# Four moves in the hand-written orders of VectorE and ScalarE in a one-layer Hymba kernel

## The chip, the cores and the metric

The kernel runs on one core of one Trainium2 chip. The metric is the device time of one execution in microseconds (us), the median of several runs. The engines are called TensorE (PE in the rows, PEld its weight loads), VectorE (DVE), ScalarE (ACT), GpSimd (POOL) and SyncE (SP, which issues DMAs).

## The reference, cut to what matters

One layer of a decoder, for 1024 rows of a new sequence and 8 rows of a cached one, in float32:

```python
h = _rmsnorm(x, g_pre_mix)
aq, ak, av, rq, rf, ri, rg = jnp.split(h @ w_in, SPLIT_POINTS, axis=-1)
...
a = _swa_prompt(q, k, v, sinks)
...
f = lb + (1.0 - lb) * jax.nn.sigmoid(rf.astype(F32))
log_f = jnp.log(f).reshape(B, T, N_REC_HEADS, REC_DK)
kr = (1.0 - f).reshape(B, T, N_REC_HEADS, REC_DK)
qr = jax.nn.silu(rq.astype(F32)).reshape(B, T, N_REC_HEADS, REC_DK)
o, S_new = _hgrn2_scan(qr, log_f, kr, ir, S0)
...
mix = jnp.concatenate([a, o], axis=-1).astype(x.dtype) @ w_out
x = x + _rmsnorm(mix, g_post_mix)
h2 = _rmsnorm(x, g_pre_ffn)
ffn = (jax.nn.silu(h2 @ w_gate) * (h2 @ w_up)) @ w_down
x = x + _rmsnorm(ffn, g_post_ffn)
```

`a` is attention over a window of 128 with a sink in the softmax (8 query heads, 2 key heads of 64). `_hgrn2_scan` is a gated linear recurrence with 4 heads of 128. `lb`, the lower bound of the forget gate, comes from a softmax over `rec_lb`. The model width is 1024, the FFN's hidden width 2816.

## The kernel before, in words

Each engine runs a program that is written out in order by hand, in loops over the same counters; semaphores connect the engines. An instruction that waits holds up everything behind it on its engine, so the order within a loop is what a change of order moves.

All large products are made of float32 numbers split in a high and a low part. ScalarE copies the high part (`copy`, L1261 in the rows), VectorE subtracts it from the number to get the low part, and TensorE multiplies high by high, high by low and low by high.

**Input projection with mixer, 132 ticks.** The projection has 22 tiles of 128 columns by 3 chunks of 344 rows, 66 units; a tick is half a unit, twelve matmuls of 128x344 (L1811). Between the ticks' matmuls TensorE takes the steps of attention and of the recurrence that the tables `attention_steps(tick)` and `recurrence_steps(tick)` name. Attention runs over 32 items; on even ticks come Q, R, E, S and M, on odd ticks PT, PV, N and D:

- S is TensorE's score product (L1886), which ScalarE copies out; D on VectorE puts in the other scores, takes the maximum and ends in `tsum` (L2448). TensorE's S of an item two later waits for that (`at_max`).
- E are ScalarE's exponentials (L1458) and `esk`; N on VectorE adds up `den` (L2452) and inverts it.
- R on ScalarE is `unit_probabilities`, the scaling of the exponentials by `rden` (L1386); PT on TensorE transposes them (L1893), PV multiplies them with the values.

The recurrence takes each of the 4 heads through a product on the diagonal ("own scores", L2486) and then seven levels, one a tick, from tick 56 + 18 h for head h. At a level VectorE runs `decay` on the queries (L2386), a masked copy of the scores out of PSUM (`copy_predicated`, L2499) and `key_step` twice (L2381); between them ScalarE moves half of the keys (`mix<-hqk` and `hqk<-hqk`, L1261). TensorE's product of the next level (L1940) waits for the decay and for the move.

Units of kind rq, rf and rg pass through gates: `unit_read` on ScalarE, at the end of odd ticks, applies the tanh (for rf with an ACT_TABLE_LOAD where the table differs, L1334) and `unit_finish` on VectorE the product (L2364, and `q_s` behind the last chunk, L2368). In a tick of VectorE come first the attention steps, then `unit_finish`, then the recurrence's steps; for heads 2 and 3 the levels come ahead of `unit_finish` (`levels_first`). The lower bound is computed in tick 27 (`lower_bound`, L2281 to L2292): three instructions on `lbt`, an Exp on ScalarE, five more instructions, and the negation of one row of `gain` (L2418), all ahead of the attention steps of that tick.

**Output projection**, then the FFN's gate and up products in a scheme of seven products per block: the list `PRODS` has 154 products of 24 matmuls of 128x258 (L2069). The first 16 are P1 and P2 of columns 0 to 7; from number 16 on they come as P6, P5, P7, P3, P4 of column 0, then of column 1 and so on. VectorE reads each product out of PSUM (`ffn_read`, L2744), which frees the pair of banks for a product three numbers later, and multiplies gate and up (`hidden`, L2751).

P6, P5, P7 and P3 work on sums of blocks of rows, split once: `sum_high` on ScalarE and `sum_low` (L2678) on VectorE, two halves each, for the four sums 2, 1, 3 and 4. TensorE waits for them at column 0 only (`s_low` 2, 4, 6 and 8). The weights are brought in as jobs X, Y, Z and W: T, T3 and T4 are sums of weights on VectorE (`weight_sums`, L2603 to L2609), `job_high` on ScalarE copies the high part, `job_low` (L2594) subtracts on VectorE. Two tables say behind which product each step comes, for both engines: `early_steps(n)` for n under 16, and `weight_steps(n)` for all others, whose entry for 16 is T4 and W of column 0.

Of the kernel before, what the change touches and what calls it, by code (L numbers as in the profile page):

```python
# [11 lines left out]
ALU = mybir.AluOpType  # L12
# [152 lines left out]
def early_steps(n):  # L165

    return {0: [("X", 2)],
# [3 lines left out]
            12: [("Y", 0), ("L", 1)], 13: [("L", 3)], 14: [("T3", 0)], 15: [("Z", 0), ("L", 4)]}.get(n, [])  # L171
# [42 lines left out]
def build(nc, t_in, t_out):  # L214
# [468 lines left out]
    def query_early(tick, i):  # L683

        return ROPE_UNITS[query_unit(i)] < tick // 2 - 2

# [572 lines left out]
    def _(act):  # L1259
# [137 lines left out]
        for tick in range(TICKS):  # L1397
# [10 lines left out]
            if tick == LB0:  # L1408
                act.wait_ge(sem("lb_step"), 1)
                act.activation(lbt[:, 2:4, :], lbt[:, 0:2, :], ACT.Exp).then_inc(sem("lb_step"), 1)  # L1410
# [26 lines left out]
            for step, i in attention_steps(tick):  # L1437
# [7 lines left out]
                elif step == "R":  # L1445
# [7 lines left out]
                elif step == "E":  # L1453
                    act.wait_ge(sem("at_max"), i + 1)
                    if i >= 2:
                        act.wait_ge(sem("at_pt"), i - 1)
                    for g in range(NKV):
                        act.activation(prob[:, e, g, :], sm[:, e, g, :], ACT.Exp, bias=negm[:, e, g:g + 1], scale=SCALE,  # L1458
                                       accum_out=den[:, e, g:g + 1])
                    act.activation(esk[:, e, :], tsum[:, e, :], ACT.Exp).then_inc(sem("at_prob"), 1)  # L1460
                elif step == "PT":
                    act.wait_ge(sem("at_pt"), i + 1)
                    if i:
                        act.wait_ge(sem("at_pv"), i)
                    copy(pt_all[:], both_groups(BP[:, 0:NKV * P])).then_inc(sem("at_ptc"), 1)
                elif step == "PV":
                    act.wait_ge(sem("at_pv"), i + 1)
                    for g in range(NKV):
                        h = slice(HD * g, HD * g + HD)
                        ins = copy(mix[h, t, P * j:P * j + P], BO[h, P * g:P * g + P])  # L1470
                    ins.then_inc(sem("at_out"), 1)
            if tick == AT0:
# [77 lines left out]
            if tick % 2:  # L1550
                for step, i in attention_steps(tick + 1):
                    if step == "Q" and query_early(tick + 1, i):
                        query_rows(i)
                unit_read(tick // 2)
# [198 lines left out]
        for n in range(2 * EARLY, NPROD):  # L1753
            ffn_reads(n)
            for name, q in weight_steps(n):
                if name in "XYZW":
                    job_high((name, q))
            if n == PIX["P7", FT - 1]:
# [462 lines left out]
    def _(dve):  # L2221
# [59 lines left out]
        def lower_bound():  # L2281
# [4 lines left out]
            dve.tensor_tensor(lbt[:, 1, :], lbl[:, 1, :], lbt[:, 4, :], ALU.subtract).then_inc(sem("lb_step"), 1)  # L2286
            dve.wait_ge(sem("lb_step"), 2)
# [119 lines left out]
        for tick in range(TICKS):  # L2407
# [7 lines left out]
            if tick == LB0:  # L2415
                lower_bound()
                dve.wait_ge(sem("g_in"), 16)
                then(dve.tensor_scalar(gain[:, PRE_FFN, :], gain[:, PRE_FFN, :], -1.0, None, ALU.mult))  # L2418
# [8 lines left out]
            for step, i in attention_steps(tick):  # L2427
# [26 lines left out]
                elif step == "M" and j:  # L2454
# [4 lines left out]
                        .then_inc(sem("at_ptp"), 1)  # L2459
            if tick == 17:  # L2460
# [5 lines left out]
            levels_first = any(step[0] == "level" and step[1] >= NREC - 2 for step in recurrence_steps(tick))  # L2466
# [424 lines left out]
        for n in range(2 * EARLY, NPROD + 1):  # L2891
            ffn_reads(n)
            for name, q in weight_steps(n):
                if name in "XYZW":
                    job_low((name, q))
                else:
                    weight_sums(name, q)
            down_steps(n)
# [86 lines left out]
```

## Time and profile before

| | |
|---|---|
| median of 3 runs | 1178.89 us (1178.26 to 1178.94) |
| the profiled execution, its own time | 1179.54 us |
| its span in the trace | 1177.8 us |
| TensorE busy | 1165.0 us, 99% of the span |
| VectorE busy | 874.2 us, 74% |
| ScalarE busy | 533.7 us, 45% |
| mean granted TensorE clock | 0.998 |

Times in the rows count from the span's start. In a timeline each row is an instruction, or several equal ones in a row (x2): its start, its length, engine, line, operation, the tiles it writes and reads with their shapes, and in brackets how long its engine had been idle before it and whose work ended that idle time. An instruction may start shortly before the one ahead of it ends. A row without brackets follows its predecessor without a wait; where the engine is TensorE, the pitch from start to start then tells more than the length, since matmuls overlap.

### The profile page before, as it was taken

To read this page: it belongs to the slowest core of one execution; us is meant where nothing else is said; L and a number is where in the kernel's file an instruction comes from. 1 tells how busy PE (TensorE), PEld (TensorE's weight loads), DVE (VectorE), ACT (ScalarE), POOL (GpSimd) and SP (SyncE) were. 2 spreads that over 40 slices of the span, in tenths; PEclk is the share of its full clock that TensorE was granted. 3 is DMA by queue.
4 is the path that set the end of the run, shared out by engine and by line. 5 is a ranking of instruction groups with operands and counts; after the bars stand their busy time and mean duration, and the time that the engine had idled before them with its cause. 6 is when DMAs were issued, how large, how long until landed. Compare 5 with 4: busy or idle time off the path is not lost.

```text
span 1177.8 us, 22993 instructions
## 1 busy us (share of the span) xinstructions
PE 1165.0 (99%) x8962; PEld 1147.4 (97%) x8962; DVE 874.2 (74%) x1493; ACT 533.7 (45%) x1192; POOL 242.2 (21%) x190
## 2 busy tenths in 40 slices
PE   9999999999999999999999999999999999999998
PEld 9999999999999999999999999999999999999997
DVE  4988587776677747799777888888887565567676
ACT  6766656745253744564222322322322235455533
POOL 1000010201120000000232365765674020000011
PEclk9999999999999999999999999999999999999999
DMA  9521101006562243253454648766864286678446
GB/s 298 144 84 34 37 19 39 19 3 125 53 157 81 84 152 94 73 158 93 138 157 153 193 162 251 234 225 224 251 233 162 101 271 189 211 255 272 147 103 118
DMA packets 173548, 170.65 MB, mean 145 GB/s; under 512 B 23064, under 2 KB 125224, under 8 KB 172912
## 3 DMA queue, kind: packets, MB, share of 16 engines
q1 hardware_dynamic: 171264, 166.00, 46.8%
q0 software_dynamic: 2176, 3.18, 1.8%
q8 instruction: 72, 1.18, 0.4%
q14 instruction: 36, 0.29, 0.1%
HBM read 117.59 MB, written 52.58 MB: 144 GB/s over the span
## 4 chain that ended last, share of the span: by engine, by line
PE 86%; DVE 7%; ACT 3%; issue 2%; DMA 1%; SPq 0%; DVEq 0%; ACTq 0%
PE pair L2069 33%; PE pair L2109 17%; PE pair L1811 16%; PE pair L2028 7%; PE pair L1940 2%; PE pair L1886 1%; PE pair L2171 1%; PE pair L1901 1%; PE pair L1905 1%; DMA mix<-x_cols_dram 1%; DVE w_lo L2594 1%; PE pair L1925 1%; DVE mix L2666 1%; DMA raw<-w_in_dram 1%; PE pair L1957 1%
## 5 line engine op out<-in xcount | busy, mean ns | idle before, releaser
L2069 PE MATMUL pair<-act_hi,w_hi 128*128 128x258 f32 x704 | 199.1, 283 | 1.1 <-DVE u_tmp L2744 1.1
L2069 PE MATMUL pair<-act_lo,w_hi 128*128 128x258 f32 x704 | 198.6, 282 | 0.0
L2069 PE MATMUL pair<-act_hi,w_lo 128*128 128x258 f32 x704 | 198.6, 282 | 0.0
L2109 PE MATMUL pair<-a_ring,w_hi 128*128 128x258 f32 x1056 | 191.6, 284 | 0.5 <-DVE mix L2804 0.4
L1811 PE MATMUL pair<-act_hi,w_hi 128*128 128x344 f32 x528 | 177.0, 335 | 0.6 <-DVE act_lo L2242 0.5
L1811 PE MATMUL pair<-act_hi,w_lo 128*128 128x344 f32 x528 | 169.2, 320 | 0.0
L1811 PE MATMUL pair<-act_lo,w_hi 128*128 128x344 f32 x528 | 168.9, 320 | 0.0
L2109 PEld LDWEIGHTS pair<-a_ring,w_hi 128*128 128x128 f32 x1056 | 163.1, 189 | 1.5 <-DVE mix L2804 0.8
L1261 ACT ACTIVATE w_hi<-rawx 128x512 fp32r<-128x512 f32 (+2 forms) x97 | 68.7, 709 | 195.9 <-PE pair L2069 84.6
L2069 PE MATMUL pair<-s_hi,w_hi 128*128 128x258 f32 x528 | 149.2, 283 | 0.5 <-DVE w_lo L2594 0.5
L2069 PE MATMUL pair<-mix_r,w_hi 128*128 128x258 f32 x528 | 149.3, 283 | 0.0
L2109 PE MATMUL pair<-a_ring,w_lo 128*128 128x258 f32 x528 | 148.9, 282 | 0.0
L2069 PE MATMUL pair<-s_hi,w_lo 128*128 128x258 f32 x528 | 148.8, 282 | 0.0
L2069 PEld LDWEIGHTS pair<-act_hi,w_hi 128*128 128x128 f32 x704 | 133.0, 189 | 1.5 <-issue 1.3
L2069 PEld LDWEIGHTS pair<-act_hi,w_lo 128*128 128x128 f32 x704 | 132.8, 189 | 0.0
L2069 PEld LDWEIGHTS pair<-act_lo,w_hi 128*128 128x128 f32 x704 | 132.7, 188 | 0.1
L1811 PEld LDWEIGHTS pair<-act_hi,w_hi 128*128 128x128 f32 x528 | 99.7, 189 | 2.1 <-DVE act_lo L2242 0.8
L1811 PEld LDWEIGHTS pair<-act_lo,w_hi 128*128 128x128 f32 x528 | 99.8, 189 | 0.8
L2069 PEld LDWEIGHTS pair<-s_hi,w_hi 128*128 128x128 f32 x528 | 99.6, 189 | 0.7 <-DVE w_lo L2594 0.7
L2109 PEld LDWEIGHTS pair<-a_ring,w_lo 128*128 128x128 f32 x528 | 100.1, 190 | 0.0
L2069 PEld LDWEIGHTS pair<-mix_r,w_hi 128*128 128x128 f32 x528 | 99.7, 189 | 0.0
L1811 PEld LDWEIGHTS pair<-act_hi,w_lo 128*128 128x128 f32 x528 | 99.6, 189 | 0.0
(382 smaller groups left out, 2629.1 us busy)
## 6 DMA issues: line engine op xcount, KB each, us to landing
raw<-w_up_dram SPq DMA_DIRECT2D x26, 512.0 KB, 5.2
a_in<-h_sums SPq DMA_DIRECT2D x44, 258.0 KB, 3.3
rawx<-w_gate_dram SPq DMA_DIRECT2D x22, 512.0 KB, 5.1
w_quarter<-w_down_dram SPq DMA_DIRECT2D x44, 256.0 KB, 3.7
w_sums<-w_quarter SPq DMA_DIRECT2D x44, 256.0 KB, 4.7
rawx<-w_sums SPq DMA_DIRECT2D x44, 256.0 KB, 4.0
raw<-w_in_dram SPq DMA_DIRECT2D x18, 512.0 KB, 4.1
h_scratch<-mix SPq DMA_DIRECT2D x23, 258.0 KB, 2.1
```

Of the source, the lines that this page charges most:

```text
L1261: return act.activation(out, in_, ACT.Copy)
L1811: mm = pe.matmul(out, a[:, k, :], b[:, k, cols(c)], start=(k == 0 and s == 0), stop=(k == KT - 1 and s == 2))
L1886: mm = pe.matmul(out[:, :, k0:], a[:, e, :], b[:, :, P * (j - 1) + k0:P * (j + 1)], start=(n == 0), stop=(n == 2))
L1901: mm = pe.matmul(out, vrow[:, j, :], pt_all[:], start=True, stop=(j == 0))
L1905: mm = pe.matmul(out, v_diff[:, e, :], pt_prev[:], start=False, stop=True)
L1925: mm = pe.matmul(pair_columns(BL[a])[:, :, c], kept[:, P * c:P * c + P], own_queries(a, c), start=True, stop=True)
L1940: mm = pe.matmul(pair_columns(BL[n % 2])[:, :, c], early_keys(h, n)[:, P * c:P * c + P], late_queries(n, c), start=True, stop=True)
L1957: mm = pe.matmul(BL[c // 4][:, P * (c % 4):P * (c % 4) + P], krow[:, c, :], irow[:, c, :], start=True, stop=True)
L2028: mm = pe.matmul(bank[(slot + 2) % 4][:, 0:QW], a[:, k, :], b[:, k, quad(slot // NOUT)], start=(k == 0 and s == 0), stop=(k == KT - 1 and ...
L2069: mm = pe.matmul(pair[psum_pair(n)][:, s, 0:QW], a[:, r, half + k, :], b, start=(k == 0 and i == 0), stop=(k == 3 and i == 2))
L2109: mm = pe.matmul(dpair(mt)[:, s, 0:a.shape[1]], b[:, cut], a, start=(m == 0 and n == 0), stop=(m == HALVES - 1 and n == 2))
L2171: mm = pe.matmul(row_bank(n), a, b[:, out], start=False, stop=(m == HALVES - 1 and i == 2))
```

## The change

Four moves on VectorE and ScalarE. The orders of TensorE, GpSimd and SyncE stay as they are, and no instruction is added or removed.

A. *Bounds in parts.* Of the lower bound the three first instructions go behind the attention steps of tick 27, ScalarE's Exp behind those of tick 28, the five others behind those of tick 29, and the row of `gain` behind those of tick 31.

B. *One level ahead of a gate's product.* `levels_first` holds for level 4 of every head, which adds heads 0 and 1, ticks 60 and 78.

C. *Probabilities' scaling ahead of the forget gate.* `scaled_early(tick)` is true two ticks behind a head's step "o". Where it is, R of the tick is run at the end of the tick before, ahead of `unit_read`.

D. *Low halves of row sums later.* In `early_steps` L2, L1 and L3 move from behind product steps 11, 12 and 13 to 12, 13 and 15, and L4 from 15 to 16, where it stands behind T4 and W. Both engines follow the table (for 16 by a line of their own).

```diff
-            8: [("S", 1, 1), ("S", 3, 1)], 9: [("X", 6), ("S", 2, 1), ("S", 4, 1)], 10: [("X", 7)], 11: [("T", 0), ("L", 2)],
-            12: [("Y", 0), ("L", 1)], 13: [("L", 3)], 14: [("T3", 0)], 15: [("Z", 0), ("L", 4)]}.get(n, [])
+            8: [("S", 1, 1), ("S", 3, 1)], 9: [("X", 6), ("S", 2, 1), ("S", 4, 1)], 10: [("X", 7)], 11: [("T", 0)],
+            12: [("Y", 0), ("L", 2)], 13: [("L", 1)], 14: [("T3", 0)], 15: [("Z", 0), ("L", 3)]}.get(n, [])
...
+    def scaled_early(tick):
+        return any(("o", h) in recurrence_steps(tick - 2) for h in range(NREC))
...
-            if tick == LB0:
-                act.wait_ge(sem("lb_step"), 1)
-                act.activation(lbt[:, 2:4, :], lbt[:, 0:2, :], ACT.Exp).then_inc(sem("lb_step"), 1)
...
-                elif step == "R":
+                elif step == "R" and not scaled_early(tick):
                     unit_probabilities(i)
...
+            if tick == LB0 + 1:
+                act.wait_ge(sem("lb_step"), 1)
+                act.activation(lbt[:, 2:4, :], lbt[:, 0:2, :], ACT.Exp).then_inc(sem("lb_step"), 1)
...
+                    if step == "R" and scaled_early(tick + 1):
+                        unit_probabilities(i)
                 unit_read(tick // 2)
...
             for name, q in weight_steps(n):
                 if name in "XYZW":
                     job_high((name, q))
+            if n == 2 * EARLY:
+                sum_high(4)
...
-            if tick == LB0:
-                lower_bound()
-                dve.wait_ge(sem("g_in"), 16)
-                then(dve.tensor_scalar(gain[:, PRE_FFN, :], gain[:, PRE_FFN, :], -1.0, None, ALU.mult))
...
+            if tick == LB0:
+                bound_exponents()
+            if tick == LB0 + 2:
+                lower_bound()
+            if tick == LB0 + 4:
+                dve.wait_ge(sem("g_in"), 16)
+                then(dve.tensor_scalar(gain[:, PRE_FFN, :], gain[:, PRE_FFN, :], -1.0, None, ALU.mult))
...
-            levels_first = any(step[0] == "level" and step[1] >= NREC - 2 for step in recurrence_steps(tick))
+            levels_first = any(step[0] == "level" and (step[1] >= NREC - 2 or step[2] == 4) for step in recurrence_steps(tick))
...
+            if n == 2 * EARLY:
+                sum_low(4)
             down_steps(n)
```

`bound_exponents` holds the first three instructions of the old `lower_bound`, which keeps the five others. Line numbers in the rows of the changed order are those of the changed kernel, some 3 to 13 higher.

VectorE in tick 60, before (the last row here begins the attention steps of the next tick):

```order
L2432 TENSOR_TENSOR q_lo<-mix,q_hi 128x128
L2364 SCALAR_TENSOR_TENSOR r_q<-th,r_q 128x344
L2368 COPY q_s<-r_q 128x8
L2386 TENSOR_TENSOR hqk<-hqk,hg 128x2x16x16
L2499 COPY_PREDICATED ast<-lmask,pair 128x2x16x16
L2381 TENSOR_TENSOR hqk<-hqk,hg 128x8x32
L2381 TENSOR_TENSOR hqk<-mix,hg 128x4x2x32
L2452 TENSOR_TENSOR den<-den,esk 128x2
```

and after:

```order
L2438 TENSOR_TENSOR q_lo<-mix,q_hi 128x128
L2396 TENSOR_TENSOR hqk<-hqk,hg 128x2x16x16
L2512 COPY_PREDICATED ast<-lmask,pair 128x2x16x16
L2391 TENSOR_TENSOR hqk<-hqk,hg 128x8x32
L2391 TENSOR_TENSOR hqk<-mix,hg 128x4x2x32
L2374 SCALAR_TENSOR_TENSOR r_q<-th,r_q 128x344
L2378 COPY q_s<-r_q 128x8
L2458 TENSOR_TENSOR den<-den,esk 128x2
```

The gate's product and `q_s` moved from ahead of the level's decay, masked copy and two key steps to behind them.

VectorE at products 11 to 16, before, from the sum L2 (into `mix_r` by `s2_hi`; L1 is `act_lo`, L3 and L4 `mix_r` by `s3_hi` and `s4_hi`; L2594 are the low parts of Y, Z and W):

```order
L2678 TENSOR_TENSOR mix_r_129<-mix_51,s2_hi_126 128x4x258 x2
L2744 TENSOR_TENSOR u_tmp_156<-v1_5_149,pair0 128x516
L2594 TENSOR_TENSOR w_lo_53<-t12_153,w_hi_52 128x1024
L2678 TENSOR_TENSOR act_lo_50<-mix_51,act_hi_49 128x4x258 x2
L2751 TENSOR_TENSOR p_small_157<-u_tmp_156,p_small_157 128x516
L2678 TENSOR_TENSOR mix_r_129<-mix_51,s3_hi_127 128x4x258 x2
L2606 TENSOR_TENSOR rawx_152<-rawx_152 128x512
L2744 TENSOR_TENSOR p_pq_159<-v1_6_150,pair0 128x516
L2594 TENSOR_TENSOR w_lo_53<-rawx_152,w_hi_52 128x1024
L2678 TENSOR_TENSOR mix_r_129<-mix_51,s4_hi_128 128x4x258 x2
L2744 TENSOR_TENSOR u_tmp_156<-v1_7_151,pair2 128x516
L2609 TENSOR_TENSOR rawx_152<-rawx_152,t12_153 128x512
```

(T4, in the last row, is followed by W's low part, L2594.) After:

```order
L2757 TENSOR_TENSOR u_tmp_156<-v1_5_149,pair0 128x516
L2607 TENSOR_TENSOR w_lo_53<-t12_153,w_hi_52 128x1024
L2691 TENSOR_TENSOR mix_r_129<-mix_51,s2_hi_126 128x4x258 x2
L2764 TENSOR_TENSOR p_small_157<-u_tmp_156,p_small_157 128x516
L2691 TENSOR_TENSOR act_lo_50<-mix_51,act_hi_49 128x4x258 x2
L2619 TENSOR_TENSOR rawx_152<-rawx_152 128x512
L2757 TENSOR_TENSOR p_pq_159<-v1_6_150,pair0 128x516
L2607 TENSOR_TENSOR w_lo_53<-rawx_152,w_hi_52 128x1024
L2691 TENSOR_TENSOR mix_r_129<-mix_51,s3_hi_127 128x4x258 x2
L2757 TENSOR_TENSOR u_tmp_156<-v1_7_151,pair2 128x516
...
L2607 TENSOR_TENSOR w_lo_53<-rawx_152,w_hi_52 128x512
L2691 TENSOR_TENSOR mix_r_129<-mix_51,s4_hi_128 128x4x258 x2
```

The read `u_tmp` is now ahead of L2, and L4 went from behind Z's low part to behind T4 and W's low part.

ScalarE at the end of tick 69, before:

```order
L1261 ACTIVATE q_hi<-mix 128x128
L1334 ACT_TABLE_LOAD
L1334 ACTIVATE r_f<-r_f 128x168
L1334 ACTIVATE r_f<-r_f 128x176
L1338 ACTIVATE r_f<-r_f,lbt 128x168
L1338 ACTIVATE r_f<-r_f,lbt 128x176
L1386 ACTIVATE prob<-prob,rden 128x128 x2
L1458 ACTIVATE prob,den<-sm,negm 128x128 x2
```

and after:

```order
L1264 ACTIVATE q_hi<-mix 128x128
L1389 ACTIVATE prob<-prob,rden 128x128 x2
L1337 ACT_TABLE_LOAD
L1337 ACTIVATE r_f<-r_f 128x168
L1337 ACTIVATE r_f<-r_f 128x176
L1341 ACTIVATE r_f<-r_f,lbt 128x168
L1341 ACTIVATE r_f<-r_f,lbt 128x176
L1458 ACTIVATE prob,den<-sm,negm 128x128 x2
```

The scaling moved ahead of the forget gate's table load and its four instructions; this is the one tick where ScalarE's order differs by C.

## Rows read from the trace of the kernel before

**Rows 1.** The page's busy times of the whole span, share of it and instruction counts.

```profile
PE 1165.0 (99%) x8962; PEld 1147.4 (97%) x8962; DVE 874.2 (74%) x1493; ACT 533.7 (45%) x1192; POOL 242.2 (21%) x190
```

**Rows 2.** Timeline of VectorE, tick 27.

```profile
start us, us, engine line op out<-in xcount [idle before <-releaser]
73.54 0.15 DVE L2284 TENSOR_TENSOR lbt<-lbl 128x4 f32<-128x4 f32 x1
...
75.60 0.16 DVE L2452 TENSOR_TENSOR den<-den,esk 128x2 f32<-128x2 f32 x1
...
76.99 0.16 DVE L2448 TENSOR_TENSOR tsum<-sink,negm 128x2 f32<-128x2 f32 x1
```

**Rows 3.** Timeline of TensorE, end of tick 27 and start of 28.

```profile
76.53 0.32 PE L1811 MATMUL pair<-act_lo,w_hi 128*128 128x344 f32 x1
76.69 0.32 PE L1811 MATMUL pair<-act_hi,w_lo 128*128 128x344 f32 x1
77.30 0.47 PE L1886 MATMUL pair<-k_hi,q_hi 128*128 128x512 f32 x1 [0.30 <-DVE tsum L2448]
```

**Rows 4.** Timeline of VectorE, tick 60 and the chain of 61.

```profile
174.65 0.52 DVE L2364 SCALAR_TENSOR_TENSOR r_q<-th,r_q 128x344 f32<-128x344 f32 x1
...
175.41 0.69 DVE L2386 TENSOR_TENSOR hqk<-hqk,hg 128x512 f32<-128x512 f32 x1
...
176.67 0.42 DVE L2381 TENSOR_TENSOR hqk<-hqk,hg 128x256 f32<-128x256 f32 x1
...
179.00 0.16 DVE L2448 TENSOR_TENSOR tsum<-sink,negm 128x2 f32<-128x2 f32 x1
```

**Rows 5.** Timeline of ScalarE, tick 60, the move of the keys.

```profile
176.24 0.40 ACT L1261 ACTIVATE mix<-hqk 128x256 f32<-128x256 f32 x1
```

**Rows 6.** Timeline of TensorE, score product of tick 62.

```profile
179.60 0.39 PE L1886 MATMUL pair<-k_hi,q_hi 128*128 128x512 f32 x1
```

**Rows 7.** Timeline of VectorE, the next level's decay behind tick 78.

```profile
246.15 0.68 DVE L2386 TENSOR_TENSOR hqk<-hqk,hg 128x512 f32<-128x512 f32 x1
```

**Rows 8.** Timeline of TensorE, the level product that reads it.

```profile
246.89 1.16 PE L1940 MATMUL pair<-hqk 128*128 128x128 f32 x8
```

**Rows 9.** Timeline of ScalarE, forget gate of tick 69 and scaling of 70.

```profile
209.17 1.28 ACT L1334 ACT_TABLE_LOAD   x1
...
211.94 0.68 ACT L1386 ACTIVATE prob<-prob,rden 128x128 f32<-128x128 f32 x2
```

**Rows 10.** Timeline of TensorE, the transposes of the probabilities.

```profile
212.68 0.44 PE L1893 MATMUL pair<-ident,prob 128*128 128x128 f32 x2 [0.56 <-ACT prob L1386]
```

**Rows 11.** Timeline of VectorE, own scores of the next head.

```profile
221.82 1.29 DVE L2486 TENSOR_TENSOR ast<-pair,ident 128x512 f32<-128x512 f32 x2 [0.26 <-PE pair L1925]
```

**Rows 12.** Timeline of VectorE, products 11 to 18: L2, u_tmp, L4, W.

```profile
535.25 2.37 DVE L2678 TENSOR_TENSOR mix_r<-mix,s_hi 128x1032 fp32r<-128x1032 f32 x2
537.54 0.69 DVE L2744 TENSOR_TENSOR u_tmp<-v,pair 128x516 f32<-128x516 f32 x1
...
547.47 2.37 DVE L2678 TENSOR_TENSOR mix_r<-mix,s_hi 128x1032 fp32r<-128x1032 f32 x2
...
551.80 0.69 DVE L2594 TENSOR_TENSOR w_lo<-rawx,w_hi 128x512 fp32r<-128x512 f32 x1 [0.76 <-ACT w_hi L1261]
```

**Rows 13.** Timeline of ScalarE, the high copies of L4.

```profile
546.20 2.01 ACT L1261 ACTIVATE s_hi<-mix 128x1032 fp32r<-128x1032 f32 x2
```

**Rows 14.** Timeline of TensorE, end of product 13, product 14, P3 of column 0.

```profile
536.96 0.28 PE L2069 MATMUL pair<-act_hi,w_lo 128*128 128x258 f32 x1
538.37 0.36 PE L2069 MATMUL pair<-act_hi,w_hi 128*128 128x258 f32 x1 [1.13 <-DVE u_tmp L2744]
...
552.87 0.28 PE L2069 MATMUL pair<-s_hi,w_hi 128*128 128x258 f32 x1
```

**Rows 15.** Timeline of TensorE, the sampled rows' products in the mixer.

```profile
318.05 1.93 PE L2000 MATMUL pair<-q_s,st 128*128 128x1 f32 x16
```

**Rows 16.** Windows: us, engines' busy time, granted TensorE clock, DMA share, GB/s.

```profile
core 0: us, PE busy (x) PEld busy (x) DVE busy (x) ACT busy (x) POOL busy (x), PEclk, DMA share, GB/s
320.40:323.00 2.60, 2.60 (x12) 2.60 (x11) 1.34 (x2) 1.16 (x2) 0.00 (x0) 0.50 1.15 38
...
536.00:539.00 3.00, 1.87 (x16) 1.70 (x15) 3.00 (x4) 3.00 (x5) 0.00 (x0) 1.00 0.92 245
```

More of the change, by code:

```diff
@@ L2279, in _, with bound_exponents @@
         row_angles(0)
-        def lower_bound():
+        def bound_exponents():
             dve.wait_ge(sem("const_in"), NCONST)
@@ L2286, in lower_bound @@
             dve.tensor_tensor(lbt[:, 1, :], lbl[:, 1, :], lbt[:, 4, :], ALU.subtract).then_inc(sem("lb_step"), 1)
+        def lower_bound():
             dve.wait_ge(sem("lb_step"), 2)
```

## The prediction

> **What bounds the kernel now.** I read the page's busy times first. TensorE is busy for 1165.0 us of a span of 1177.8, VectorE for 874.2, ScalarE for 533.7 [rows 1]. All that better order can give back is therefore TensorE's idle time, 12.8 us in several pieces, and each part of this change must be judged at one place: which wait ends last there, and what is late behind it. So I read the timelines of the engines around each place that the diff names, and look in each for two things: a bracket, which says that an engine stood still and for whom, and the slack between an instruction's end and the start of the one that needs it.
>
> The profiled execution took 1179.54 us, 0.65 above the median of the runs, 1178.89. I make the sum against 1179.54 and carry the difference over to the median. A measurement of this kernel can tell about 0.2% (2.36 us) from no change; "same" below means within that.
>
> **Part A, bounds in parts (ticks 27 to 31).** In tick 27 VectorE's nine small instructions, eight on lbt and one on gain, stand from 73.54 to 75.60 ahead of den and of the softmax chain that ends in tsum at 76.99 + 0.16 = 77.15 [rows 2]. TensorE's score product waits for that chain: it starts at 77.30 with 0.30 idle, though the matmul ahead of it started at 76.69 and the pitch there is 0.16 [rows 3]. With eight of the nine behind the chain, and the three of tick 27 behind it too, the chain ends up to 75.60 - 73.54 = 2.06 earlier, and the score product starts at 76.69 + 0.16 = 76.85. That is **-0.45**. The bracket alone gives -0.30 for the other end. The exponential on ScalarE moves behind a score copy and the five remaining VectorE instructions go into tick 29, behind the chain of that tick. By the share of five in nine of those 2.06 they take about 1.1 us, and VectorE enters tick 28 about 2 us ahead, which covers them. If that cover were gone they would give back those 0.45 at the next score product, no more.
>
> **Part B, one level ahead of a gate's product (ticks 60 and 78).** Here VectorE runs r_q's gate product and q_s (174.65 to 175.41, 0.76 us) ahead of the level's decay, masked copy and two key steps [rows 4]. The change puts the 0.76 us behind the key steps, as the order shows. What does the level win? Its first key step starts at 176.67, right when ScalarE's move of the keys (176.24 + 0.40 = 176.64) is done [rows 4, 5]. ScalarE does not wait for VectorE's decay there, so the key step stays at 176.67: the decay and the copy end 0.76 earlier, and VectorE then stands idle for that time. The 0.76 us come after the key steps instead, ahead of den and the chain to tsum. Tsum ended at 179.00 + 0.16 = 179.16 [rows 4], and now ends at 179.93. The score product of tick 62 starts at 179.60 without a bracket [rows 6]; with the 0.15 from tsum's end to the product that rows 2 and 3 show (77.15 to 77.30) it can start at 180.08. That is **+0.48** for head 0; without any slack it would be +0.77.
>
> In tick 78 the pattern repeats for head 1, and the work that ends last is the next level's decay: it starts at 246.15, and with its 0.68 us ends at 246.83 [rows 7]; TensorE's level product starts at 246.89 [rows 8], so nothing lies between. The 0.77 goes through whole: **+0.77**, or +0.5 if TensorE finds the slack that it had for head 0. A gain would need the decay or the copy to be what somebody waits for in these two ticks, and no row here shows that.
>
> **Part C, probabilities' scaling ahead of a forget gate.** The order of ScalarE differs in one place only, tick 70: the title's second tick has no scaling step. There the scaling (0.68) starts at 211.94, behind a table load of 1.28 us and the gate's four instructions that began at 209.17 [rows 9]. TensorE's transposes wait for it, 0.56 us [rows 10]. Moved ahead of the table load, it is done 2.8 us sooner and the wait is gone. But ScalarE's exponentials stay where they are: the gate, put 0.68 later, ends when the scaling ended before. So all that hangs on the exponentials, the next score product's chain among it, comes no sooner, and TensorE runs into it. Later VectorE's own scores, at 221.82, waited for TensorE for 0.26 [rows 11]; what TensorE gains beyond that VectorE no longer follows. I take that row, **-0.26**, between 0 (VectorE and ScalarE decide everything behind) and -0.56 (the whole bracket).
>
> **Part D, low halves of the row sums later (products 11 to 20).** L2, L1, L3 and L4 are pairs of VectorE subtractions, 2.37 us a pair (pitch 2.29); each needs a pair of copies on ScalarE of 2.01 us [rows 12, 13]. Before, L2 began at 535.25, and the read u_tmp that frees a PSUM pair stood behind it at 537.54 [rows 12]. Product 14 waited for that read: it starts at 538.37, where its predecessor's last matmul started at 536.96 and the pitch is 0.12 [rows 14]. So 1.41 - 0.12 = 1.29 is lost, and the change removes it: u_tmp starts at 535.25, TensorE does not wait, and every later product is due 1.29 earlier. P3 of column 0, which needs L4, was at 552.87 [rows 14] and is due at 551.58.
>
> What is late next is L4. Before, it started at 547.47 and was over at 549.84, 3.0 us ahead of P3 [rows 12, 14]. Now it stands behind T4 and the weights' low part W, whose w_lo started at 551.80 [rows 12]. Taking L4's pitch of 2.29 out ahead of it, w_lo starts at 549.51 at the earliest, and L4, 0.61 later (w_lo takes 0.69 and the next instruction starts 0.08 before its end), ends at 550.12 + 2.37 = 552.49: already 0.9 behind P3's new due time. It will be later than that, because L2 also filled VectorE's wait for ScalarE's high copy of Y, which now shows: w_lo of W, with nothing to fill its wait, stood 0.76 idle [rows 12], and I take 0.67 for Y: that 0.76 less the 0.09 by which an instruction starts before its predecessor's end. So w_lo of W starts at 549.51 + 0.67 = 550.18, and ScalarE, whose copy of W's high part has to be over before that, can begin L4's two high copies at about 550.05 and ends them 2.01 later, at 552.06 [rows 13]. The second subtraction, half of 2.37, then runs from about 552.3 to 553.5, and with the 0.15 to TensorE P3 starts at 553.65 instead of 552.87. Behind a wait TensorE's first matmul takes 0.08 longer (0.36 against 0.28 [rows 14]). So the wait of 1.29 at product 14 goes and one of about 2.1 at P3 takes its place: **+0.85**. The bounds are -0.24 (L4 ends at 552.49, P3 at 552.63) and +1.2 (L3, for which I find 0.36 us of slack, is late too). Queued behind L4 on VectorE are the reads of the main loop; they start about when they did before relative to TensorE, so I charge nothing for them.
>
> **The sum.** -0.45 + 0.48 + 0.77 - 0.26 + 0.85 = **+1.4 us**: the profiled 1179.54 becomes 1180.93, the median 1178.89 becomes **1180.3**. TensorE's own queue, POOL's and SP's are in the same order before and after, and no DMA is moved, so nothing else is charged. With each bound at its low end the sum is -0.30 + 0.48 + 0.5 - 0.56 - 0.24, about -0.1; at its high end -0.30 + 0.77 + 0.77 + 0 + 1.2 = 2.4. Against the median that is 1178.8 to 1181.3, the forecast's own range.
>
> **The rivals.**
> 1. **L4 is in time and D pays whole.** If ScalarE runs ahead more than I replay, P3 is not held and D is -1.29. Sum -0.75: **1178.1**. For it speaks that L4 had 3.0 us to spare; against it, that the earliest end by rows is already behind the due time.
> 2. **B costs nothing.** If the keys are moved earlier than at 176.24, the key steps come sooner and the 0.76 fits in. The sum without B's 1.25 is +0.14: **1179.0**. Against it: ScalarE's queue ahead of that move is not touched.
> 3. **All four do what they say.** -0.45 - 0.26 - 1.29 and B nothing is -2.0, with C whole -2.3: **1176.6 to 1176.9**, the edge of what counts as faster. It needs rivals 1 and 2 at once.
> 4. **Slower: TensorE's clock falls at P3.** In the stretch from 320.40 to 323.00, soon after sixteen matmuls of one column that took 1.93 us [rows 15], the granted clock is 0.50 (1.2 GHz); from 536 to 539, around the wait of 1.13 at product 14, it is 1.00 (2.4 GHz) [rows 16]. The new wait at P3 is about 2.1, longer than the one at product 14. If the clock falls for as long as it did there, 2.60 us at half speed lose 1.30, and the time is **1181.6**, slower by over 0.2%. It decides if the chip answers the wait at P3 as it answered the stretch of small matmuls and not as it answered product 14. The Trainium skill says on "TensorE: Matmul & The Clock Gate", in "A second HAM failure mode: psum-queue depth-cycling", that small idles between groups of matmuls can be enough to bring the lower level back again and again. By that rule the time would be this rival's; the trace does not bear it out at product 14.
>
> **Chances.** Forecast 0.43; rival 1 0.17; rival 2 0.16; rival 3 0.11; rival 4 0.13. Rival 3 is left out of the range, and so is what lies above rival 4's time: 1177.6 to 1181.7. Faster by over 0.2% (below 1176.53) is about two thirds of rival 3, 0.07. Slower (above 1181.25) is most of rival 4, 0.11, and the upper tail of the forecast, 0.03: 0.14. The rest, 0.79, is within 0.2%.
>
> **What would show it.** A is right if the score product near 77 us has no bracket. B is wrong if the key step of tick 60 starts before 176.6, right if VectorE idles some 0.8 us ahead of it and the score product and the level product come later by 0.5 and 0.8. C is right if the transposes near 212 us have no wait. D is right if product 14 starts without a wait and P3 of column 0 shows about 2 us of waiting for mix_r; it is wrong if P3 has none, and rival 4 holds if the granted clock behind P3 is 0.50.

## The result, and the profile after

The changed kernel takes 1181.27 us (median of 18 runs, 1179.06 to 1182.76), the kernel before on the same chips 1179.13 (18 runs, 1177.86 to 1181.57): the medians lie 2.1 us apart. The ratio on record is **1.0015, 95% interval 1.0009 to 1.0021**, 1.8 us (1.1 to 2.5) slower. The forecast was 1.4 us slower and within 0.2%. The profiled execution took 1181.22, its span 1179.4 against 1177.8.

Busy times of the changed kernel, and what TensorE waited for (engine, line and work waited for: us in all, times, longest):

```profile
PE 1165.5 (99%) x8962; PEld 1147.9 (97%) x8962; DVE 871.1 (74%) x1493; ACT 533.9 (45%) x1192; POOL 243.1 (21%) x190
```

```profile
PE pair L2076 <- DVE mix_r L2691: 2.0, 1, 2.0
PE pair L1947 <- issue: 2.0, 3, 0.8
PE pair L1824 <- DVE neg L2276: 1.1, 1, 1.1
PE pair L1947 <- DVE hqk L2396: 0.8, 1, 0.8
```

TensorE's busy time is within 0.5 us of what it was [rows 1]; what differs is its waits. Before, it had 1.13 for u_tmp and 0.56 for the probabilities [rows 14, 10]. Both are gone, and two others stand there: 2.0 for mix_r, which is L4, and 0.8 for the decay of a level, which is B.

To see where each part paid or cost, I took the start of every TensorE matmul in a profiled execution and subtracted the start of the same matmul in that of before. This difference runs level over long stretches and steps at a few places. The table gives the steps in us (negative is gained): the level behind a place less the level ahead of it, each the median over the matmuls of the stretch. It has the changed kernel and most of the experiments below ("first keys" and "next keys" are TensorE's two waits of 0.8 at the levels near 169 and 236). Steps under 0.1 us, a step of 0.2 near 534 in B alone, those of the first 45 us, where every execution differs, and what a lower clock near 320 to 350 cost or spared some executions are left out.

| place (us in the trace of before) | changed | B alone | D alone | L4 back | read alone, A, C | + keys, B | + keys, T | + keys, T, B |
|---|---|---|---|---|---|---|---|---|
| 77, A | -0.53 | 0 | 0 | -0.53 | -0.53 | -0.53 | -0.53 | -0.53 |
| 168, first keys | 0 | 0 | 0 | 0 | 0 | -0.81 | -0.81 | -0.82 |
| 172, behind them | 0 | 0 | 0 | 0 | 0 | +0.13 | +0.14 | +0.13 |
| 179, B of head 0 | +0.54 | +0.55 | 0 | +0.56 | 0 | 0 | +0.19 | 0 |
| 186, in every kernel | +0.32 | +0.30 | +0.29 | +0.31 | +0.28 | +0.28 | +0.31 | +0.27 |
| 212, C | -0.78 | 0 | 0 | -0.78 | -0.78 | -0.78 | -0.78 | -0.78 |
| 215 and 231, given back | +0.52 | 0 | 0 | +0.53 | +0.57 | +0.52 | +0.54 | +0.55 |
| 235, next keys | 0 | 0 | 0 | 0 | 0 | -0.82 | -0.82 | -0.82 |
| 239 and 247, B of head 1 | +0.78 | +0.78 | 0 | +0.78 | 0 | +0.15 | +0.55 | +0.13 |
| 340, a load | 0 | +1.12 | 0 | +0.84 | +2.77 | +3.01 | +1.66 | 0 |
| 537 and 541, product 14 | -1.39 | 0 | -1.39 | -1.36 | -1.16 | -1.20 | -1.21 | -1.23 |
| 553, P3 (product 19) | +2.28 | 0 | +2.26 | 0 | 0 | 0 | 0 | 0 |
| 558, product 21 | 0 | 0 | 0 | +1.62 | +0.76 | +0.80 | +0.19 | +0.19 |
| 594 and 616 | 0 | 0 | 0 | +0.82 | 0 | 0 | 0 | 0 |
| 645 to 651 | -0.56 | -0.60 | -0.52 | -0.52 | -0.60 | -0.52 | -0.73 | -0.73 |

The steps of the changed kernel that belong to its four parts add up to -0.53 + 0.54 - 0.78 + 0.52 + 0.78 - 1.39 + 2.28 = +1.4. The rows at 186 and 645 stand in every kernel, also in D alone, whose order is that of before up to product 11, near 530: they belong to the one profiled execution of before and not to the change. They and the row at 340 are taken up in the last section.

The lines that answer to [rows 2, 3], VectorE and TensorE at A's place: the chain to tsum runs first, lbt behind it, and the score product follows the pitch without a bracket.

```profile
74.98 0.45 DVE L2454 TENSOR_TENSOR tsum<-sink,negm 128x2 f32<-128x2 f32 x1
75.35 0.15 DVE L2291 TENSOR_TENSOR lbt<-lbl 128x4 f32<-128x4 f32 x1
...
76.59 0.32 PE L1818 MATMUL pair<-act_hi,w_lo 128*128 128x344 f32 x1
76.75 0.39 PE L1893 MATMUL pair<-k_hi,q_hi 128*128 128x512 f32 x1
```

Those that answer to [rows 4 to 8], VectorE, ScalarE and TensorE at B's places:

```profile
174.52 0.72 DVE L2512 COPY_PREDICATED ast<-lmask,pair 128x512 f32<-128x512 uint8 x1
176.05 0.42 DVE L2391 TENSOR_TENSOR hqk<-hqk,hg 128x256 f32<-128x256 f32 x1 [0.81 <-ACT mix L1264]
...
177.00 0.50 DVE L2374 SCALAR_TENSOR_TENSOR r_q<-th,r_q 128x344 f32<-128x344 f32 x1
...
175.61 0.40 ACT L1264 ACTIVATE mix<-hqk 128x256 f32<-128x256 f32 x1
...
179.44 0.47 PE L1893 MATMUL pair<-k_hi,q_hi 128*128 128x512 f32 x1 [0.30 <-DVE tsum L2454]
...
247.68 0.49 PE L1947 MATMUL pair<-hqk 128*128 128x128 f32 x2 [0.81 <-DVE hqk L2396]
```

VectorE idles 0.81 ahead of the key step of tick 60, until ScalarE's move (175.61 + 0.40) is done; the gate's product follows the key steps, and the score product and the level product both have a wait that they did not have.

Those that answer to [rows 9 to 11], ScalarE, VectorE and TensorE from C's place to the score product near 231:

```profile
209.32 0.69 ACT L1389 ACTIVATE prob<-prob,rden 128x128 f32<-128x128 f32 x2
...
213.67 0.36 ACT L1264 ACTIVATE sm<-pair 128x256 f32<-128x256 f32 x1
...
213.79 0.16 DVE L2458 TENSOR_TENSOR den<-den,esk 128x2 f32<-128x2 f32 x1 [3.93 <-ACT esk L1460]
...
214.07 0.44 DVE L2449 COPY_PREDICATED sm<-tri,pair 128x256 f32<-128x256 int32 x1
...
221.86 1.28 DVE L2499 TENSOR_TENSOR ast<-pair,ident 128x512 f32<-128x512 f32 x2
...
230.58 0.16 DVE L2454 TENSOR_TENSOR tsum<-sink,negm 128x2 f32<-128x2 f32 x1
...
212.23 0.38 PE L1900 MATMUL pair<-ident,prob 128*128 128x128 f32 x2
...
215.50 0.47 PE L1893 MATMUL pair<-k_hi,q_hi 128*128 128x512 f32 x1
...
230.89 0.47 PE L1893 MATMUL pair<-k_hi,q_hi 128*128 128x512 f32 x1
```

The transposes have no wait. The softmax chain behind them starts with den, which waits 3.93 for the exponentials' last step as it did before, and its copy of the scores (sm, done at 213.67 + 0.36 = 214.03) is ready only 0.04 before the chain takes it up.

Those that answer to [rows 12 to 14], VectorE, ScalarE and TensorE from W to P3:

```profile
550.99 0.69 DVE L2607 TENSOR_TENSOR w_lo<-rawx,w_hi 128x512 fp32r<-128x512 f32 x1 [0.76 <-ACT w_hi L1264]
551.95 2.38 DVE L2691 TENSOR_TENSOR mix_r<-mix,s_hi 128x1032 fp32r<-128x1032 f32 x2 [0.26 <-ACT s_hi L1264]
...
550.86 2.01 ACT L1264 ACTIVATE s_hi<-mix 128x1032 fp32r<-128x1032 f32 x2
...
537.87 0.28 PE L2076 MATMUL pair<-act_hi,w_hi 128*128 128x258 f32 x1
...
554.47 0.36 PE L2076 MATMUL pair<-s_hi,w_hi 128*128 128x258 f32 x1 [2.03 <-DVE mix_r L2691]
```

Product 14 starts at 537.87 without a wait. L4 ends at 551.95 + 2.38 = 554.33, and P3 starts 0.14 later.

### The profile page after: what moved, and what is told of

It reads as the page before. It is cut to its first block, busy times and chain, and to the rows that moved or that the text cites. A ratio compares the mean times of both kernels' runs of the same rounds, so it can differ in the third digit from the quotient of the medians.

```text
span 1179.4 us, 22993 instructions
## 1 busy us (share of the span) xinstructions
PE 1165.5 (99%) x8962; PEld 1147.9 (97%) x8962; DVE 871.1 (74%) x1493; ACT 533.9 (45%) x1192; POOL 243.1 (21%) x190
## 4 chain that ended last, share of the span: by engine, by line
PE 82%; DVE 9%; ACT 4%; issue 2%; DMA 1%; SPq 0%; DVEq 0%; ACTq 0%
PE pair L2076 33%; PE pair L2116 17%; PE pair L1818 14%; PE pair L2035 7%; PE pair L2178 1%; PE pair L1947 1%; PE pair L1893 1%; DVE w_lo L2607 1%; DMA mix<-x_cols_dram 1%; PE pair L1908 1%; PE pair L1912 1%; DVE mix L2679 1%; DVE hqk L2391 1%; DMA raw<-w_in_dram 1%; PE pair L1964 1%
```

## The experiments

Each kernel is the one named with the edit shown. Times are medians beside runs of the kernel before on the same chip; the steps by place are in the table.

**D alone.** The kernel before with the change's lines of `early_steps`, `sum_high(4)` and `sum_low(4)` only.

> Kernel before with part D alone. Theory (the read moved ahead removes one wait, L4 behind W makes another): the wait of 1.13 at product 14 is gone, and P3 of column 0 waits about 2.0 us for mix_r, as in the changed kernel; TensorE is 1.3 ahead between the two and about 0.8 behind after P3; the time is 0.5 to 0.9 us over that of before. Rival (B's and C's delays upstream are what makes L4 late): without them P3 waits under 1 us and the time is at least 0.5 us under before.

Measured: ratio 1.0005 (0.9994 to 1.0016). By place it is what the theory says: -1.39 at product 14, then 2.02 of waiting for mix_r, +2.26. That is +0.87, with nothing upstream changed, so the rival falls. The runs alone do not decide it: their interval, 0.7 us under to 1.9 over, holds the theory's 0.5 to 0.9 over and the rival's 0.5 under.

**B alone.** The kernel before with one line:

```diff
-step[1] >= NREC - 2 for step
+(step[1] >= NREC - 2 or step[2] == 4) for step
```

> Kernel before with part B alone. Theory (the gate's product now stands between the key steps and the softmax chain, and nothing waited for the level): the key step of tick 60 starts no sooner than 0.03 after ScalarE's move of the keys, with some 0.8 us of VectorE idle ahead of it, TensorE loses 0.4 to 0.5 at the score product near 179.6, some 0.2 to 0.3 at the next near 186 and 0.8 at the level product near 246.9; the time is about 1.4 us over before. Rival (B is covered, and the loss of the changed kernel is all D's): the time is within 0.4 us of before.

Measured: ratio 1.0010 (1.0000 to 1.0021). By place +0.55 at the score product near 179 and +0.78 at the level product, 1.33 in all, so the rival falls. The +0.30 at the next score product, near 186, is not B's: D alone has +0.29 there.

**L4 back ahead of W.** The changed kernel with

```diff
-15: [("Z", 0), ("L", 3)]}
+15: [("Z", 0), ("L", 3), ("L", 4)]}
```

and without its two lines for 16.

> The changed kernel with only L4 put back behind L3, ahead of T4 and W, on both engines. Theory (the place of L4 in the two queues makes the wait at P3): product 14 has no wait, P3's wait shrinks from 2.0 to under 0.3, and the time is 1.3 to 2.0 us under that of the changed kernel. Rival (VectorE has too much to do between products 11 and 19, whatever its order): P3, P7 or P4 waits 1 us or more instead, and the time is within 0.7 us of the changed kernel.

Measured: ratio 1.0009 (0.9999 to 1.0019), so no gain on the changed kernel's 1.0015 that the intervals show. P3 has no wait, as the theory says, but product 21 does, for the low part of Y of column 1:

```profile
560.19 0.39 PE L2074 MATMUL pair<-s_hi,w_hi 128*128 128x258 f32 x1 [1.33 <-DVE w_lo L2605]
```

Another 0.8 is lost near 594 and 616. L4's place makes the wait at P3, and yet the rival had the time right: in this order too VectorE has more to do from product 14 to 21 than there is time for, and the wait is handed on.

**Less work for VectorE.** The kernel just shown, with L1's low halves taken for the first of four blocks of rows; the other three quarters are left out.

```diff
-1: (mix[:, 4:8, rows], act_hi[:, 0:4, rows], act_lo[:, 0:4, rows]),
+1: (mix[:, 4:5, rows], act_hi[:, 0:1, rows], act_lo[:, 0:1, rows]),
```

> The kernel with L4 put back ahead of T4 and W (the run before of that kind waited 1.3 us for Y's low part at product 21), and with L1's two subtractions on a quarter of their rows' blocks, so that VectorE has about 1.6 us less to do between products 12 and 21; three quarters of L1's low halves are left out. Theory (from product 14 on VectorE's queue is full to product 21, so a wait only moves along it): the wait at product 21 is under 0.2 us and no other appears between products 14 and 21. Rival (Y of column 1 is late for ScalarE or a load, not for VectorE's work): the wait at product 21 stays above 1 us.

Measured in one execution: no wait of TensorE is left between product 14 and product 21; the step at product 14 stays whole, -1.36. So it was the amount of work in VectorE's queue that made product 21 wait, and the theory stands. (The time of this one execution, 1186.8, is that of the wait near 340 and a fall of the clock behind it.)

**Only the read ahead of L2, with A and C, without B.** The kernel before with A, C and

```diff
-11: [("T", 0), ("L", 2)], 12: [("Y", 0), ("L", 1)],
+11: [("T", 0)], 12: [("L", 2), ("Y", 0), ("L", 1)],
```

> Kernel before with A, C and another form of D: only the read of product 11 goes ahead of L2, all four sums otherwise in the places of before; B left out. Theory: A gives 0.45, C 0.2 to 0.3, the read 1.3 and P3 has no wait, 2.0 us in all at that point; further on, the wait of 0.6 at the product near 645 may grow, since VectorE does not come sooner there. The time is 1.0 to 2.2 us under before. Rival (a wait further on takes all of it back): within 0.6 us of before.

Measured: ratio 0.9995 (0.9981 to 1.0009), undecided. By place A (-0.53), C (-0.21) and the read (-1.16) give about what was expected and P3 has no wait, but product 21 gives back 0.76 (L4 back had a wait there too), and in the profiled execution a wait of 2.6 near 340, which stands in other kernels too, took more than all of it.

**Exponentials ahead of the gate as well.** The changed kernel, with E of tick 70 run behind R at the end of tick 69.

> The changed kernel, with ScalarE's exponentials of tick 70 moved ahead of the forget gate too, behind the scaling. Theory (C's gain is cut at the next score product because the exponentials stay behind the gate): the score product near 215.5 has no wait any more, where the changed kernel gave back 0.23; the gain of 0.6 at the transposes stays. Rival (the copy of the scores or VectorE's chain behind cuts it): the score product near 215.5 gives back 0.2 as in the changed kernel.

Measured in one execution: the theory falls. TensorE gives back 0.40 at the score product near 215, as the changed kernel does (0.38), and VectorE shows for whom it waits now:

```profile
212.40 0.17 DVE L2469 RECIPROCAL rden<-den 128x2 f32<-128x2 f32 x1
213.93 0.45 DVE L2459 COPY_PREDICATED sm<-tri,pair 128x256 f32<-128x256 int32 x1 [1.36 <-ACT sm L1264]
```

The reciprocal behind den comes 1.6 us sooner than in the changed kernel, and then the chain waits for ScalarE's copy of the scores, the third step that stands behind the gate. In the changed kernel the exponentials and this copy are ready almost together, so moving the exponentials alone gains nothing; the copy alone was not tried.

**All three ahead of the gate.** The same with S of tick 70 ahead too.

> The changed kernel with all of ScalarE's attention steps of tick 70 ahead of the forget gate: scaling, exponentials and score copy. In the run with only the exponentials ahead VectorE waited 1.36 us for the score copy. Theory (the score copy behind the gate is what cuts C's gain): the score product near 215.5 gives back under 0.1; the chain on VectorE of the head behind decides again near 230.7, where 0.2 to 0.5 is given back. Rival (the gate, now 1 us later, holds its own readers): TensorE shows a new wait between 212 and 225.

Measured in one execution: the score product near 215 gives back nothing (+0.02), and C's -0.78 is held to 220, but then +0.15 before 225, +0.38 at the transposes near 228 and +0.32 at the score product near 231 take all of it back. The theory on the copy stands. By place C's net gain is -0.26 in the change and -0.25 with the exponentials ahead, and there is none with all three ahead (+0.09). This execution also shows rival 4 of the prediction (below).

**Keys moved early, with B.** The kernel with A, C and the read alone; ScalarE runs its move of the keys of levels 2 and 4 just ahead of E instead of behind the attention steps; and B.

```diff
 elif step == "E":
+    for other in recurrence_steps(tick):
+        if other[0] == "level" and moved_early(tick, other[2]):
+            key_move(other[1], other[2])
```

> Kernel before with A, C, the read alone ahead of L2, and B, and with ScalarE's move of the keys ahead of the exponentials at the levels 2 and 4. Theory (B lost because the key step waits for that move in ScalarE's queue; and the two waits of 0.8 at the levels near 169 and 236 are that move as well): with B the key step of tick 60 starts 0.6 to 0.8 sooner than in the changed kernel, B's losses at the score products near 179 and 186 and at the level product near 247 shrink to under 0.3 in all, and the two waits near 169 and 236 lose 0.6 or more each. Rival (VectorE's gate product ahead of the softmax chain is what costs, whenever the keys come): B's losses stay at 1.2 or more.

Measured in one execution (its time of 1183.17 holds the wait near 340 and a fall of the clock behind it): the two waits near 169 and 236 are gone (-0.81, -0.82), and the +0.54 at 179 and the +0.78 at 247 that B cost are gone as well. VectorE's key step follows the copy without a wait:

```profile
174.03 0.72 DVE L2521 COPY_PREDICATED ast<-lmask,pair 128x512 f32<-128x512 uint8 x1
174.64 0.40 DVE L2400 TENSOR_TENSOR hqk<-hqk,hg 128x256 f32<-128x256 f32 x1
```

What is left, 0.13 near 172, 0.28 at 186 and 0.15 near 239, is over the 0.3 that was expected, but it stands in the next kernel too, which has no B. The rival falls: the move of the keys was what the levels waited for.

**Keys early and T a product earlier, without B.** The kernel with A, C, the read alone and the keys early, and in `weight_steps`

```diff
-plan = {-3: ("T", "Y"), -1: ("T3", "Z"), 0: ("T4", "W")} if q else
+plan = {-4: ("T",), -3: ("Y",), -1: ("T3", "Z"), 0: ("T4", "W")} if q else
```

> Kernel before with A, C, the read alone ahead of L2, ScalarE's move of the keys ahead of the exponentials at the levels 2 and 4, without B, and with the weights' sum T of columns 1 to 7 one product earlier than Y, so that VectorE has a read to do while ScalarE copies Y's high part. Theory: A 0.45, C 0.2, the keys 1.2 to 1.6, the read 1.2, and the wait at product 21 that the read alone brought (0.5 to 0.7) is gone; 2.5 to 3.5 us under before, less up to 0.7 further on. Rival (VectorE's full queue gives back the read's 1.2 further on, and the keys' gain is cut by the chains behind): less than 1.2 us under before.

Measured: ratio **0.9980 (0.9971 to 0.9989)**, 2.4 us (1.3 to 3.4) under before. That is just under the 2.5 that the theory had at the least, and the rival, less than 1.2, falls. Product 21 gives back 0.19 instead of 0.76: with a read between T and Y VectorE stands still for 0.59 instead of 1.19 while ScalarE copies Y's high part.

**The same with B.**

> The kernel that was 0.2% faster (A, C, the read alone ahead of L2, keys moved early on ScalarE at the levels 2 and 4, T a product earlier) with B added. Theory (once the keys come early B no longer waits, and spares TensorE the 0.5 at the level product near 247): by place the losses at 172, 180, 186 and 247 fall from 1.1 to about 0.5; 0.4 to 0.7 us under that kernel apart from the wait near 340, that is 2.5 to 3.5 us under before. Rival (B costs 1.2 wherever it stands): about 1.2 us over that kernel.

Measured: ratio **0.9974 (0.9963 to 0.9985)**, 3.1 us (1.8 to 4.4) under before, the fastest kernel here. From 172 to 247 TensorE loses 0.54, where the kernel without B loses 1.19: with the keys early B gains 0.6, where in the change it costs 1.3. The interval overlaps that of the kernel without B, so between these two the places decide, not the runs.

**The same with tick 70's steps ahead of the gate.**

> The same kernel with ScalarE's attention steps of tick 70 all ahead of the forget gate. Theory: like it, and 0.2 us less at the score product near 215; 2.5 to 3.7 us under before. Rival (given back near 230.7): equal to it within 0.2 us by place.

Measured: ratio 0.9984 (0.9975 to 0.9993). By place -0.78 at 212, nothing at 215, and +0.36 and +0.33 at 228 and 231: the rival is right, the gain is given back there.

## Why the forecast held, point by point

*Part A* was forecast at -0.45, and the score product's first matmul comes 0.45 sooner. The step is -0.53, since the first matmul behind a wait takes 0.08 longer; the prediction counted that 0.08 in D, and not in A and B. A's remainder, moved to ticks 29 and 31, shows up nowhere.

*Part B*: the mechanism is right in each step: the key step waits for ScalarE's move, VectorE idles 0.81 (0.76 forecast), the gate's product falls into the softmax chain. Head 0 was forecast at +0.48 and is +0.54, the same 0.08 included; head 1 was forecast at +0.77 and is +0.78. *Rival 2*, that B costs nothing, was bound to a key move earlier than 176.24; in the changed kernel it is not, and with the move made earlier B did pay.

*Part C* was forecast at -0.26 and is -0.78 + 0.52 = -0.26. The mechanism is the one forecast: den still waits for the exponentials, so 0.38 is given back at the score product near 215. The rest follows VectorE, whose queue shows no wait from 221.86 to tsum at 230.58. Before, VectorE had idled 0.26 for TensorE at 221.82 [rows 11]; that idle stretch is gone, it was all that VectorE could win, and at 231 TensorE gives back what it had beyond that. Two things were missed without harm. The gain at the transposes is more than the bracket of 0.56, which the prediction took for the most that there was. And the copy of the scores holds the chain as long as the exponentials do, within 0.04.

*Part D*: -1.29 and a wait of about 2.1 were forecast, +0.85 together; product 14's first matmul came 1.29 sooner and TensorE waited 2.03 at P3, and by place it is -1.39 + 2.28, about +0.9. The replay of VectorE's queue, with a wait of 0.67 at Y, put P3 at 553.65 in the times of before, and it came at 554.47, or about 553.7 less the 0.8 by which TensorE was late by then; Y's wait turned out 0.59.

*Rivals 1 and 3*, which need L4 in time, fall with the wait at P3.

*Rival 4*, the clock: behind P3, which started at 554.47, the granted clock is 1.00 in the profiled execution of the changed kernel (553.5 to 556.5), and in those of D alone and of the exponentials' kernel. But in one of the four with this wait, where all three steps stand ahead of the gate and TensorE waited 1.96 us there, it did fall. The windows, first of the changed kernel, then of that execution ahead of P3's start and behind it (columns as in [rows 16]):

```profile
553.50:556.50 3.00, 2.03 (x17) 2.06 (x18) 3.00 (x5) 0.00 (x0) 0.00 (x0) 1.00 0.03 12
...
553.00:556.50 3.50, 1.62 (x14) 1.41 (x12) 3.13 (x4) 1.98 (x3) 0.00 (x0) 1.00 0.00 0
557.00:560.00 3.00, 3.00 (x17) 3.00 (x16) 2.54 (x5) 0.33 (x1) 0.00 (x0) 0.51 0.36 106
```

By place that cost 1.5 us (the difference ended at +5.3, where the wait alone would have left it at +3.8; forecast 1.30). So the rival is no single outcome: it comes in some executions. How often, four profiles can't tell.

By place the four parts make +1.4, as forecast, each within 0.1. The 1.8 of the runs (1.1 to 2.5) agrees with that; what more there may be, no place shows. One slip stands in the sum of the low bounds: it takes A at -0.30, where A's low end is -0.45, so that sum is -0.3 and not -0.1; the range does not hang on it.

## What to carry to other kernels

A wait is removed only when the work behind it has room: list what each engine's queue must finish by which product, and if the sum is short, moving one item hands the wait on, as L2's went to P3, then to product 21; less work ended it, and a filled idle stretch (T ahead of Y) took all but 0.2 of it. Before putting a step earlier, find who it waits for: B cost 1.3 us while ScalarE's key move stood behind the exponentials, and gained 0.6 once that was moved. And where effects are below a measurement's spread, compare traces matmul by matmul: A's -0.53 and C's -0.78 repeated to 0.01 in all ten kernels that have them, while the runs of one kernel spread over 4. Look for each step in a kernel without the edit too: one that stands there belongs to the trace compared with.

## What the runs showed that I had not expected

**A load near 340 decides up to 3 us.** TensorE waits there between 0 and 3.0 us longer than in the profile of before, whatever the edit. In the kernel with the read alone, SyncE's store of the states holds its queue for 10.13 us (2.29 before), the load of ib goes out behind it at 330.02 (327.05 before), and VectorE waits for that load:

```profile
318.04 10.13 SPq L956 DMA_DIRECT2D st_p_out<-states  x1
328.21 0.43 SPq L852 DMA_DIRECT2D raw<-w_in_dram  x1
330.02 0.33 SPq L932 DMA_DIRECT2D ib<-i_sample  x1
```

```profile
336.15 1.14 DVE L2568 SCALAR_TENSOR_TENSOR vs<-ib,k_s,vs 128x128 f32<-128x128 f32 x4 [3.81 <-DMA ib<-i_sample]
```

The store's hold alone does not decide it. In the fastest kernel it held the queue for 9.08, the load went out at 327.71, and TensorE did not wait; in B alone it held it for 2.53, the load went out at 331.38, and TensorE waited 0.97. What makes the store take 1 us in one execution and 10 in another, and what else holds the load, stays open; another order of these transfers was not tried. After a wait of 2.87 there the clock fell as well, in the kernel with the keys early and B (and after one of 2.43 in the one with less work, but not after the one of 2.62 with the read alone). That execution lacks the fall that all others have between 318 and 331, so it may be the same fall, come later. The window, with the columns of [rows 16]:

```profile
345.00:350.00 5.00, 5.00 (x20) 5.00 (x21) 2.27 (x4) 0.82 (x2) 0.00 (x0) 0.50 0.00 0
```

The Trainium skill states on "TensorE: Matmul & The Clock Gate", in "A second HAM failure mode: psum-queue depth-cycling", that small idles can bring the lower level back; here the clock fell behind three of the seven waits of 1.96 to 2.87 us, once at P3 and twice near 340, and not behind the other four.

**GpSimd holds up VectorE instructions.** The steps at 186 and 645 come from two VectorE instructions that ran beside GpSimd. Near 184 den took 0.16 in the profile of before, where it started in the same hundredth as GpSimd's v_diff; in all twelve others it took 0.30 to 0.47 and ended within 0.02 of v_diff, and the score product behind it came 0.3 later. That delay is there with B and without. The first two lines are of before, the others of D alone:

```profile
184.24 0.16 DVE L2452 TENSOR_TENSOR den<-den,esk 128x2 f32<-128x2 f32 x1
184.24 0.49 POOL L1170 TENSOR_TENSOR v_diff<-vrow 128x128 f32<-128x128 f32 x1 [6.83 <-PE pair L1905]
```

```profile
184.01 0.46 DVE L2454 TENSOR_TENSOR den<-den,esk 128x2 f32<-128x2 f32 x1
184.00 0.46 POOL L1170 TENSOR_TENSOR v_diff<-vrow 128x128 f32<-128x128 f32 x1 [6.82 <-PE pair L1907]
```

At 645 the luck was on the other side: near 621 T4 took 1.73 us in before while GpSimd added two tiles; in the changed kernel it took 0.69, having started 0.10 ahead of GpSimd. The first two lines are of before, the others of the changed kernel:

```profile
621.25 1.73 DVE L2609 TENSOR_TENSOR raw<-raw,t 128x512 f32<-128x512 f32 x1
621.14 1.30 POOL L1224 TENSOR_TENSOR e_buf<-mix,p_z 128x516 f32<-128x516 f32 x1 [4.06 <-DMA h_sums<-e_buf]
```

```profile
622.95 0.69 DVE L2622 TENSOR_TENSOR raw<-raw,t 128x512 f32<-128x512 f32 x1
623.05 1.75 POOL L1227 TENSOR_TENSOR e_buf<-mix,p_z 128x516 f32<-128x516 f32 x1 [4.26 <-DMA h_sums<-e_buf]
```

VectorE's chain to product 51 came 1 us late by it, and TensorE waited 0.45 there; no other execution here shows that wait. No run moved GpSimd's instructions, so that they are the cause is read from the overlap and was not tested. It agrees with the Trainium skill, "GPSIMD Engine Reference", "1. Specifications", by which GpSimd and VectorE share their way into SBUF and get in each other's way when a VectorE instruction has two inputs there.
